# The first blocks of a linear, multiplied block by block or tile by tile

## The reference, cut to what matters

```
h = rms_norm(x, w) * (1.0 + scale) + shift          # 1024 features
y = h @ w_in                                        # even_in, gdn_w_in, w_in of the second network
y = square(relu(h @ w1)) @ w2                       # first network's feed-forward
y = (silu(h @ w_gate) * (h @ w_up)) @ w_down        # second network's feed-forward
```

## Time and profile before

| | |
|---|---|
| median of three runs | 2140.6 us (2140.32 to 2144.93) |
| the profiled execution | 2143.72 us, its span 2141.9 us |
| mean granted PE clock | 0.982 of full |
| PE busy | 2035.5 us (95%), 16840 matmuls |
| PE weight loads | 1784.0 us (83%) |
| DVE busy | 1519.6 us (71%) |
| ACT busy | 907.4 us (42%) |
| HBM read | 320.84 MB, 150 GB/s over the span |

### The profile page before, as it was taken

One profiled execution on the slowest core, in us unless ns is written; L12 is line 12 of the kernel. 1 busy time (PEld: TensorE's weight loads), 2 busy tenths in 40 slices (PEclk: granted clock), 3 DMA queues, 4 the chain that ended last, 5 costly groups with the idle time before them and its releaser, 6 DMA issues. The chain is left out here.

```text
span 2141.9 us, 40191 instructions
## 1 busy us (share of the span) xinstructions
PE 2035.5 (95%) x16840; PEld 1784.0 (83%) x16840; DVE 1519.6 (71%) x2353; ACT 907.4 (42%) x1355; POOL 142.3 (7%) x231
## 2 busy tenths in 40 slices
PE   7999989999999989999999999999999999999997
PEld 5787766788888678789888999889799978988997
DVE  6875557798776668766646777789767667966544
ACT  2435553222222244432225444556544445554443
POOL 0100000001010011210220000000000000000000
PEclk7999999999999999999999999999999999999999
DMA  8542013455454176200003777443357744323552
GB/s 328 205 148 79 2 60 138 137 179 213 161 197 152 59 270 209 97 3 3 3 3 132 247 271 284 159 168 119 138 204 278 275 147 158 138 99 130 185 182 93
DMA packets 59133, 323.94 MB, mean 151 GB/s; under 512 B 6384, under 2 KB 7536, under 8 KB 32624
## 3 DMA queue, kind: packets, MB, share of 16 engines
q1 hardware_dynamic: 33360, 228.97, 30.0%
q0 software_dynamic: 25344, 92.29, 12.2%
q10 hardware_dynamic: 288, 0.66, 0.1%
HBM read 320.84 MB, written 1.05 MB: 150 GB/s over the span
## 5 line engine op out<-in xcount | busy, mean ns | idle before, releaser
L370 DVE TENSOR_TENSOR w_low<-raw,w_high 128x1024 fp32r<-128x1024 f32 (+1 forms) x408 | 473.6, 1202 | 196.2 <-ACT w_high L362 195.9
L362 ACT ACTIVATE w_high<-raw 128x1024 fp32r<-128x1024 f32 (+1 forms) x408 | 402.6, 1034 | 367.2 <-PE banks L407 355.9
L405 PE MATMUL banks<-ffn_a_l,w_high 128*128 128x256 f32 x704 | 199.6, 283 | 4.7 <-DVE ffn_hidden L1109 1.9
L406 PE MATMUL banks<-ffn_a_h,w_high 128*128 128x256 f32 x704 | 197.7, 281 | 0.0
L407 PE MATMUL banks<-ffn_a_h,w_low 128*128 128x256 f32 x704 | 197.7, 281 | 0.0
L548 DVE SCALAR_TENSOR_TENSOR mod_rows<-mod_rows,silu_condition 128x1024 f32<-128x1024 f32 x162 | 195.9, 1221 | 2.6 <-ACT silu_condition L451 1.0
L405 PE MATMUL banks<-mlp_hidden_l,w_high 128*128 128x512 f32 (+1 forms) x512 | 173.9, 340 | 2.7 <-DVE mlp_y L1126 2.7
L407 PE MATMUL banks<-mlp_hidden_h,w_low 128*128 128x512 f32 (+1 forms) x512 | 174.0, 340 | 0.0
L406 PE MATMUL banks<-mlp_hidden_h,w_high 128*128 128x512 f32 (+1 forms) x512 | 173.8, 339 | 0.0
L534 POOL DMA_DIRECT2D mod_rows<-rows_dram x162 | 85.8, 530 | 1257.8 <-DVE mod_rows L548 1044.0
L405 PEld LDWEIGHTS banks<-ffn_a_l,w_high 128*128 128x128 f32 x704 | 132.6, 188 | 9.5 <-issue 5.3
(11 more groups left out here) (622 smaller groups left out, 5039.6 us busy)
## 6 DMA issues: line engine op xcount, KB each, us to landing
raw<-panels_dram SPq DMA_DIRECT2D x204, 1024.0 KB, 4.8
mod_rows<-rows_dram POOLq DMA_DIRECT2D x162, 512.0 KB, 5.1
mod_0a_rows<-rows_dram SPq DMA_DIRECT2D x8, 1024.0 KB, 19.8
odd_k_tok<-rows_dram POOLq DMA_DIRECT2D x14, 512.0 KB, 5.0
x_features<-x_features_dram SPq DMA_DIRECT2D x1, 2048.0 KB, 11.5
constants<-small_dram SPq DMA_DIRECT2D x1, 1672.5 KB, 7.0
silu_condition<-conditions_dram SPq DMA_DIRECT2D x2, 512.0 KB, 12.7
out_dram<-x_features SPq DMA_DIRECT2D x4, 256.0 KB, 2.1
```

The costliest lines, as they stand in the source:

```text
L362: self.nc.scalar.activation(self.wh[:, m % 2, cols], self.raw[:, slot, cols], ACT.Copy).then_inc(self.w_high, 1)
L370: self.nc.vector.tensor_tensor(self.wl[:, m % 2, cols], self.raw[:, slot, cols], self.wh[:, m % 2, cols].bitcast(F32), ALU.subtract).then_ ...
L405: self.nc.tensor.matmul(out, sh(k), ml(k), start=(opens and k == 0), stop=False)
L406: self.nc.tensor.matmul(out, sh(k), mh(k), start=False, stop=False)
```

## The change

`product3` gets a parameter `only`: with it, it issues the triple of one tile alone. `linear` gets `together`, the number of blocks that are multiplied side by side. With `together` = n, PE first waits for the splits of all the panels that hold these n blocks, then goes tile by tile: wait for tile k, then the triples of tile k of all n blocks, each into its own bank. From block n on it is as before. `odd_g` has `together=4` (two panels), both `mix_in` have `together=2` (one panel). In the feed-forwards `pe_up` does the same for the two blocks of the first panel, which means in `mlp0` and in both `ffn`; `up_done` is raised, as before, after both blocks. Nothing is changed on DVE, ACT, POOL and SP, and the number of matmuls is the same.

```diff
--- before.py
+++ after.py
@@ -396,10 +396,10 @@
     def wait_split(self, pe, m, q=None):
         pe.wait_ge(self.w_split, self.in_loop(lambda x: 2 * x + 2, m, q))
 
-    def product3(self, out, sh, sl, mh, ml, nk, opens=True, closes=True):
-
-
-        for k in range(nk):
+    def product3(self, out, sh, sl, mh, ml, nk, opens=True, closes=True, only=None):
+
+
+        for k in range(nk) if only is None else [only]:
             if self.operand_wait is not None:
                 self.operand_wait(k)
             self.nc.tensor.matmul(out, sh(k), ml(k), start=(opens and k == 0), stop=False)
@@ -811,9 +811,7 @@
 
     def linear(self, name, panels, per_panel, nblocks, product, evac, x_ready, engines=("dve", "act"),
                banks=(0, 1, 2, 3), after=(), beside=None, rising=False, prior=None, info=None, carry=True, first_out=None,
-               behind=None):
-
-
+               behind=None, together=0):
 
 
         nc, nb = self.nc, len(banks)
@@ -835,7 +833,20 @@
         def _(pe):
             for w in x_ready if not rising else []:
                 pe.wait_ge(*w)
-            for q in range(nblocks):
+            for p in range(together // per_panel):
+                if beside is not None:
+                    beside("pe", pe, p)
+                self.wait_split(pe, ms[p])
+            for q in range(together):
+                if prior is not None and banks[q] in prior["bank_free"]:
+                    pe.wait_ge(*prior["bank_free"][banks[q]])
+            for k in range(KD if together else 0):
+                pe.wait_ge(x_ready[0][0], k + 1)
+                for q in range(together):
+                    last = product(q, ms[q // per_panel], self.ps[:, banks[q], :], k)
+                    if k == KD - 1:
+                        last.then_inc(done, 1)
+            for q in range(together, nblocks):
                 m = ms[q // per_panel]
                 if q % per_panel == 0:
                     if beside is not None:
@@ -883,11 +894,11 @@
     def features(self, high, low, n, nk, offset, order=None):
         order = list(range(nk)) if order is None else order
 
-        def product(q, m, bank):
+        def product(q, m, bank, only=None):
             at = lambda k: slice(offset(q, order[k]), offset(q, order[k]) + P)
             return self.product3(bank[:, 0:n],
                                  lambda k: self.wh[:, m % 2, at(k)], lambda k: self.wl[:, m % 2, at(k)],
-                                 lambda k: high[:, order[k], 0:n], lambda k: low[:, order[k], 0:n], nk)
+                                 lambda k: high[:, order[k], 0:n], lambda k: low[:, order[k], 0:n], nk, only=only)
         return product
 
     def narrow(self, high, low, n, width, nk):
@@ -1045,14 +1056,20 @@
                 m = m_of["up", cs, u]
                 if u == 0 and cs >= (1 if gated else 2):
                     pe.wait_ge(h_ready, c)
-                for b in range(2):
-                    if cs == 0 and u == 0 and b == 0:
-                        self.operand_wait = lambda k: pe.wait_ge(a_ready[0][0], k + 1)
-                    last = self.product3(ps[:, 2 * u + b if gated else up_banks(cs).start + b, 0:n],
+                def product(b, only=None):
+                    return self.product3(ps[:, 2 * u + b if gated else up_banks(cs).start + b, 0:n],
                                          lambda k: self.wh[:, m % 2, k * PC + b * P:k * PC + (b + 1) * P],
                                          lambda k: self.wl[:, m % 2, k * PC + b * P:k * PC + (b + 1) * P],
-                                         lambda k: high[:, k, 0:n], lambda k: low[:, k, 0:n], KD)
-                    self.operand_wait = None
+                                         lambda k: high[:, k, 0:n], lambda k: low[:, k, 0:n], KD, only=only)
+
+                if cs == 0 and u == 0:
+                    for k in range(KD):
+                        pe.wait_ge(a_ready[0][0], k + 1)
+                        for b in range(2):
+                            last = product(b, k)
+                else:
+                    for b in range(2):
+                        last = product(b)
                 last.then_inc(up_done, 1)
 
         def pe_down_kept(pe, cs, q=None):
@@ -1946,7 +1963,7 @@
     pr.busy_before(4, 6)
     g_info, ab_info, v_info, qk_info = {}, {}, {}, {}
     g_ready = pr.linear("odd_g", 4, 2, 8, pr.features(high, low, TL, KD, tall_offset),
-                        pr.copy_out(lambda q: gate[:, q, :]), a_ready, info=g_info, rising=True,
+                        pr.copy_out(lambda q: gate[:, q, :]), a_ready, info=g_info, rising=True, together=4,
                         beside=lambda which, eng, p: beside(which, eng, 1 + p // 2))
     ab_ready = pr.linear("odd_ab_in", 1, 1, 1, pr.narrow(high, low, N, 32, KD),
                          lambda q, which, eng, bank: nc.scalar.activation(pre[0:32, 7, :], bank[0:32, :], ACT.Copy), [],
@@ -2888,7 +2905,7 @@
 
     pr.busy_before(3, 7)
     pr.linear("mix_in", 4, 2, 8, pr.features(high, low, N, KD, tall_offset), block_out(0), a_ready,
-              engines=who[:8], rising=True, beside=beside_first, info=a_info, first_out=conv_first(0))
+              engines=who[:8], rising=True, together=2, beside=beside_first, info=a_info, first_out=conv_first(0))
     sm_t = work[0:32, 0, :]
     pr.linear("mix_small_in", 1, 1, 1, pr.narrow(high, low, N, 32, KD),
               lambda q, which, eng, bank: nc.scalar.activation(sm_t, bank[0:32, 0:N], ACT.Copy), [],
```

## The result

The changed kernel takes 2151.03 us in the median of five runs (2148.38 to 2151.53), the kernel before 2140.6, now of five runs too (2139.71 to 2144.93). The ratio is 1.0041, with a 95% interval from 1.0027 to 1.0055: slower by 8.8 us, or 5.8 to 11.8. The forecast was +4.0 with a range up to +8.9. The profiled execution of the new kernel is the fastest of its five (2148.38, span 2146.6, clock 0.981), so the two traces differ by only 4.7 us; the rest is spread among executions, to which the experiments come back.

The account below looks back on a forecast made before the run. PE, busy 95% of the span, was taken to bound the kernel. Terms for `mlp0`, `odd_g`, `ffn` and mixers, -4.4 + 9.2 - 0.4 - 0.4 = +4.0, on 2140.6 gave 2144.6 us, range 2140.0 to 2149.5.

Parts of the forecast that it names:

- mlp0: Layer 1's feed-forward: triples at PE's own pace end earlier, gain 4.4 us (3.4 to 5.0), carried on behind it.
- odd_g, first wait: PE waits for the second panel's split, starts `odd_g` at 767.0 at the lower clock for 3.4 us, costing 1.5.
- a first triple of `odd_g` before 762: Sign that would show the forecast wrong; PE's first triple was expected at about 762.5, with times 4.4 earlier.
- odd_g, second wait: Ahead of block 4 PE stands 3.2 us for the third panel's split; blocks 4 to 7 take 11.4 plus 1.3.
- Nothing takes the loss up: Behind `odd_g` PE is busy 104.23 of 105 us, so 9.2 stays; rival that it is absorbed: 8 in 100.
- Mixers: First linears of both mixers: second panel is late, gain 0 in the first and 0.4 us in the second.
- ffn: Both `ffn`: second panel's split limits the gain to 0.2 us each, 0.4 in all.
- this wait can bring the lower clock, for 1.5 us: In `ffn`, PE's wait of about 1.9 us for the second panel; ends +0.4 and -1.1, 0.2 taken.
- The sum: Whole kernel: -4.4 + 9.2 - 0.4 - 0.4 = +4.0 us, giving 2144.6.
- the forecast's own 2141 to 2148.5: Range of the main forecast without rivals, +0.5 to +7.9 us; its chance is 78 in 100.
- one difference of 3.1 us between an execution and the median: Runs' median 2140.6 is 3.1 us below the profiled 2143.72; the same difference was laid on 2147.7.
- A change of accumulator with every triple: Rival: 112 bank changes over the six places cost 0.1 us each, 11 us, for 2156; chance 3 in 100.

Follow-up runs that it names:

- e2: Kernel before with only `odd_g` changed, its four blocks side by side: 2150.94 us, ratio 1.0044.
- g2: Kernel before with only the two `ffn` changed, plus two filler matmuls ahead of the second panel: 2141.58 us, ratio 0.9996 to the kernel before.
- g1: As e2, but 15 filler matmuls instead of 4 ahead of `odd_g`: 2151.37 us, ratio 1.0041 to the kernel before.
- e4: Kernel before with only the two `ffn` changed, without fillers in the wait: 2145.88 us, ratio 1.0013.
- g3: Kernel before with only the two mixers' first linears changed: 2142.91 us, ratio 1.0001.
- e3: Kernel before with only `odd_g` changed, two blocks (one panel) side by side instead of four: 2141.85 us, ratio 0.9996.
- f3: As e2, but 46 filler matmuls instead of 4 ahead of `odd_g`: 2177.49 us, ratio 1.0159 to the kernel before.

## Why the prediction was nearly right, and where it was not

*mlp0.* Right: the stretch is 4.49 us shorter (forecast 4.4), PE waits for no tile after the first, and the gain carries. By time it is 3.0, with an interval (1.1 to 4.9) that holds both.

*odd_g, first wait.* Right in place and kind. PE starts at 760.00, and the forecast of 767.0 moved by the trace's shift of -6.96 is 760.0. By the prediction's own sign, "a first triple of `odd_g` before 762", this would be wrong; but that time reckoned with a shift of 4.4 from `mlp0` alone, and the other 2.5 us in the ledger are no part of the change. The four blocks took 13.25 us instead of 12.9, since the lower clock held for 4.2 us and not 3.4.

*odd_g, second wait.* Right: from 773.25 (0.12 behind the last matmul's start) to 776.52 it is 3.3 us. Blocks 4 to 7 took 13.0 instead of 12.7, with the clock at 0.50 for 3.4 us. In all the trace has 9.8 where the sum had 9.2, and e2 measured 9.4. The waits were read rightly; the lengths of the low stretches were estimates that came near, and e2's trace has no fall behind the second wait at all.

*Nothing takes the loss up.* Right: PE is busy for 104.23 us of the 105 behind the linear, exactly as before.

*Mixers.* Right: 0 and 0.35, forecast as 0 and 0.4. The new waits for the second panel were 0.74 and 1.50 us, the first shorter than the 1.5 to 2 forecast.

*ffn.* Wrong in sign. The step that failed is "this wait can bring the lower clock, for 1.5 us; so the ends are +0.4 and -1.1, and I take 0.2". Both traces show the fall in both `ffn` (+1.04 and +1.25 in the ledger of the whole change), and alone they cost 2.8 us by time (0.9 to 4.7). The term is +2.8 instead of -0.4. The mechanism was named there, with its size nearly right (+1.1 for one `ffn`); what failed is that it was taken for the exception. g2 shows the cause: with PE at work in the wait, the loss is gone.

*The sum.* With the measured parts it is -3.0 + 9.4 + 2.8 + 0.2 = 9.4 instead of 4.0; `ffn` makes 3.2 of the difference, `mlp0` 1.4, the mixers 0.6 and `odd_g` 0.2. That three of the four terms and the way came out is no luck, but that the total still fell inside the range is in part: the range allowed a fall in one `ffn` only. The median of 2151.03 lies outside the range, the ratio on 2140.6 (2149.4) just within, and outside the forecast's own 2141 to 2148.5. (The chances as given add up to 0.49 for slower and 0.08 for faster, not 0.48 and 0.09.) One more thing was too narrow. I took one difference of 3.1 us between an execution and the median and laid it on the sum. But 75 runs of the kernel before, in the three groups, spread from 2139.5 to 2150.0 us with a standard deviation of 2.1, and their mean granted clock goes from 0.980 to 0.988: by a straight line through them, a clock lower by 0.001 goes with 0.74 us. A term of one or two us, read from one trace, carries this spread, and the traces' difference of 4.7 us against 8.8 in the runs lies within it. Which stretches differ from run to run isn't known, since only one execution of each is profiled; the one of 1.55 us in the ledger is an example between kernels.

## What to carry to other kernels

Before a group of products is taken side by side to fill waits for one operand, list what else they need together: here four blocks needed a second panel of weights, whose split stood behind the norm in DVE's stream, and freed both slots at once at the end. Side by side pays as far as the operands that are already there reach: by the traces 4.5 us in `mlp0`, where two panels were; 2.7 in `odd_g` with one, more than half of it by a clock that did not fall (an estimate, and not to be told from nothing in the time); and next to nothing or a loss in the mixers and `ffn`, where the next panel was ready only half a microsecond before PE had come to it block by block. And a gain that ends in a new wait of PE can be worth less than the timeline says, since the clock can fall behind it: it did behind 1.8 us in `ffn`, and not behind 1.5 in the second mixer. Two filler matmuls inside that wait of `ffn` kept it up; read a filler's duration from the trace first.

## What the runs showed of the hardware that was not expected

A change of accumulator with every triple costs nothing that these traces show: in the new kernel's `mlp0` sixteen triples of 512 columns, alternating between two banks, took 11.24 us, or 0.70 each, as they did when one bank was kept for eight of them. In `odd_g` it was four banks: in g1, at full clock, its 32 triples took 11.5 us, which is 32 of 0.356 and 0.1 for the restart.

Behind PE's waits of 1.8 us for the second panel in `ffn`, the granted clock was 0.50 for 3.4 us, at both such waits of the whole change and at both of e4. Behind the waits of 1.5 us in the second mixer (whole change and g3) and of 1.64 us in e3 it was 1.00. The waits of 0.4 us for tiles in `mlp0` of the kernel before, six in a row behind one of 0.83, had no such stretch between them; from the third of the four of 0.7 to 0.9 us in its `odd_g` on, it had one of 6.8 us. So the length of one wait alone does not tell whether the clock falls. The Trainium skill ("TensorE: Matmul & The Clock Gate", section "HAM oscillation — how this bites in real kernels") warns of such falls behind waits for data, in a kernel with longer waits, for DMA. The traces agree on the fall, and have it behind waits of 1.8 us for DVE's split too. The advice that goes with it there for thin products, to do all contraction tiles of one output before PE waits for data again, was right for `odd_g` with four blocks and a late panel, and for `ffn` without fillers. It was wrong for `mlp0`, where the opposite order gained 4.49 us, and by the traces for `odd_g` with two blocks, where the opposite order was the one with the clock at 1.00.

A filler matmul in plain float32 with 512 columns takes 0.86 us at full clock: its two records in the profile start 0.43 us apart in f3's trace (87 records in the 37.0 us from 756.0 on, at clock 1.00). The 0.90 above is the mean of 46, of which the first ran at 0.50 for 3.4 us. Counting records gives twice the number of these matmuls. A product's matmul of the same width, whose operands are rounded, takes 0.23 us (0.70 for three).
